# Recurrence of a hybrid encoder layer on one core: the two directions' 64x64 products placed in different quarters of the matmul array, alternating by units, and the outputs' first terms issued ahead of the state's update

## What is computed

```python
def rwkv7_step(S, inp):
    r, w, k, v, a, b = inp
    sa = jnp.einsum('dbhvk,dbhk->dbhv', S, a)
    S = S * w[..., None, :] + sa[..., None] * b[..., None, :] + v[..., :, None] * k[..., None, :]
    y = jnp.einsum('dbhvk,dbhk->dbhv', S, r)
    return S, y
...
    S0 = jnp.zeros((N_DIRS, B, H, N, N), jnp.float32)
    _, y = lax.scan(rwkv7_step, S0, xs)
    y = jnp.moveaxis(y, 0, 2)
    y = y[0] + jnp.flip(y[1], axis=1)
```

## Time and profile before

| | us |
|---|---|
| median of three runs | 3061.29 |
| lowest, highest | 3059.34, 3065.22 |
| profiled execution, first to last instruction (its span) | 3048.9 |

### The profile page before, as it was taken

The page is one execution under the profiler, slowest core; times in us unless marked ns, Lnnn a source line. Parts: engine busy times, 40 slices in busy tenths (PEclk is TensorE's granted clock), DMA queues, the critical chain, the costliest instruction groups (busy, mean ns, idle before and its releaser), DMA issues. The chain is left out here.

```text
span 3048.9 us, 62296 instructions
## 1 busy us (share of the span) xinstructions
PE 2789.9 (92%) x24610; PEld 2226.5 (73%) x24610; DVE 2058.0 (68%) x3096; ACT 1363.4 (45%) x2618; POOL 665.4 (22%) x843
## 2 busy tenths in 40 slices
PE   7889989998659999996999789999799999799999
PEld 4655578884459999994667678888588888588887
DVE  6867623235586666634446878888888888587786
ACT  4547711116635555543244434455444454344443
POOL 5447700000037787721232000000000000000000
PEclk9999999999869999998999899999899999899999
DMA  4432222324794444334654132222122221726401
GB/s 131 149 94 50 49 80 68 77 55 162 286 285 148 139 144 143 95 110 160 193 176 152 68 116 77 83 83 80 56 83 80 83 77 66 278 98 225 158 28 56
DMA packets 302490, 361.25 MB, mean 118 GB/s; under 512 B 119977, under 2 KB 202409, under 8 KB 302082
## 3 DMA queue, kind: packets, MB, share of 16 engines
q1 hardware_dynamic: 297314, 352.01, 35.6%
q10 hardware_dynamic: 4896, 5.38, 0.5%
HBM read 254.16 MB, written 103.14 MB: 117 GB/s over the span
## 5 line engine op out<-in xcount | busy, mean ns | idle before, releaser
L99 PE MATMUL up_p<-up_b_hi,up_a_hi 128*128 128x512 f32 x1232 | 490.3, 398 | 43.2 <-ACT inv L2295 23.3
L100 PE MATMUL up_p<-up_b_lo,up_a_hi 128*128 128x512 f32 x1232 | 490.1, 398 | 0.0
L101 PE MATMUL up_p<-up_b_hi,up_a_lo 128*128 128x512 f32 x1232 | 489.6, 397 | 0.0
L99 PEld LDWEIGHTS up_p<-up_b_hi,up_a_hi 128*128 128x128 f32 x1232 | 233.7, 190 | 103.7 <-ACT inv L2295 24.6
L100 PEld LDWEIGHTS up_p<-up_b_lo,up_a_hi 128*128 128x128 f32 x1232 | 233.6, 190 | 56.0
L101 PEld LDWEIGHTS up_p<-up_b_hi,up_a_lo 128*128 128x128 f32 x1232 | 233.5, 189 | 55.4
L2738 ACT CAST down_a_hi<-down_a 128x512 fp32r<-128x512 f32 x154 | 96.0, 623 | 259.5 <-PE down_p_x L101 143.4
L2250 ACT CAST up_a_hi<-up_a_sum 128x512 fp32r<-128x512 f32 x132 | 81.4, 617 | 224.3 <-DVE up_a_sum L2409 147.3
L2753 DVE TENSOR_TENSOR down_a_lo<-down_a,down_a_hi 128x512 fp32r<-128x512 f32 x154 | 106.3, 690 | 97.5 <-ACT down_a_hi L2738 97.5
L2320 ACT ACTIVATE up_con<-up_raw,vecs_sb 128x1023 f32<-128x1023 f32 (+1 forms) x88 | 109.7, 1246 | 127.4 <-DVE up_raw L2479 83.9
L2485 DVE SCALAR_TENSOR_TENSOR up_con<-up_raw,vecs_sb,up_con 128x1023 f32<-128x1023 f32 (+1 forms) x88 | 113.1, 1285 | 65.9 <-ACT up_con L2320 65.9
(11 more groups left out here) (298 smaller groups left out, 7356.9 us busy)
## 6 DMA issues: line engine op xcount, KB each, us to landing
up_a_raw<-in_w_up SPq DMA_DIRECT2D x172, 256.0 KB, 2.7
rec_inp<-gate_chunks SPq DMA_DIRECT2D x64, 512.0 KB, 3.7
down_a<-in_w_down SPq DMA_DIRECT2D x88, 256.0 KB, 8.7
down_b<-act_out SPq DMA_DIRECT2D x88, 256.0 KB, 9.0
first_w<-in_w_attn SPq DMA_DIRECT2D x24, 512.0 KB, 3.5
rkv_chunks<-rwkv_project_mix SPq DMA_DIRECT2D x12, 1024.0 KB, 6.5
gate_chunks<-gates_out SPq DMA_DIRECT2D x3, 4096.0 KB, 12.2
act_out<-up_con SPq DMA_DIRECT2D x22, 512.5 KB, 2.6
```

The costliest lines, as they stand in the source:

```text
L99: pe.matmul(out, w_hi, x_hi, start=start, stop=False, skip_group_check=True)
L100: pe.matmul(out, w_hi, x_lo, start=False, stop=False, skip_group_check=True)
L101: return pe.matmul(out, w_lo, x_hi, start=False, stop=stop, skip_group_check=True)
```

## The change

In PE's part of the recurrence `pair` gets an argument `across`, which exchanges the output's halves: partitions 0 to 63 in go to 64 to 127 out and the other way round, that is, to the two quarters off the diagonal. `x_part`, `u_part` and `gram` become `x_parts`, `u_parts` and `grams`: in each, direction 0 lies on the diagonal and direction 1 off it, and the directions alternate unit by unit. All waits of both directions stand ahead of the first matmul. `y_part` is cut in two: `y_given` (the terms from the values and from H) ahead of `h_part`, and `y_solved` (the term from u) behind it; here direction 0 lies off the diagonal and direction 1 on it. `tok_b_part` and `tok_part` become `tok_parts`, called with 0 ahead of `cross` and with 1 behind it: each call turns b of one direction (diagonal) and k of the other (off it), alternating. The semaphore `tok` is now `tok_k`, and `tok_copy` on ACT waits for both `tok_b` and `tok_k`. Since direction 0's outputs now come out with their halves exchanged, the mix loads them in two DMAs of 64 partitions in place of one of 128, and `sums` waits for three DMAs in place of two. The number and the shapes of the matmuls are the same, and the orders on ACT, DVE and POOL are as before.

```diff
-                def pair(to, lhs, rhs, start=True, stop=True):
-                    for rows in HALVES:
-                        mm = pe.matmul(to[rows], lhs[rows], rhs[rows], start=start, stop=stop)
+                def pair(to, lhs, rhs, start=True, stop=True, across=0):
+                    for h, rows in enumerate(HALVES):
+                        mm = pe.matmul(to[HALVES[h ^ across]], lhs[rows], rhs[rows], start=start, stop=stop,
+                                       skip_group_check=True)
                     return mm
...
-                def x_part(c, d):
...
+                def x_parts(c):
+                    for d in DIRS:
+                        done(pe, "ak_masked", d, c + 1)
+                        done(pe, parity("v", c), d, 48 * (c // 2 + 1))
+                        done(pe, "h_added", d, c)
+                        done(pe, "h_decayed", d, c)
                     for u in range(RU):
                         if c > 0:
-                            pair(to[:, u], ar[d][:, c % RING, u, 0:L], H[d][:, c % 2, u], True, False)
-                        mm = pair(to[:, u], akrk[d][:, c % 2, u, 0:L], vtok[d][:, c % 2, u], c == 0, True)
-                    mm.then_inc(S["x"][d], 1)
-                def u_part(c, d):
-                    done(pe, "merged", d, c + 1)
-                    done(pe, "x_copied", d, c + 1)
-                    each(bank[d][0][:, :, 0:L], Z[d], xs[d]).then_inc(S["u"][d], 1)
+                            for d in DIRS:
+                                pair(bank[d][0][:, u, 0:L], ar[d][:, c % RING, u, 0:L], H[d][:, c % 2, u], True,
+                                     False, across=d)
+                        for d in DIRS:
+                            mm = pair(bank[d][0][:, u, 0:L], akrk[d][:, c % 2, u, 0:L], vtok[d][:, c % 2, u],
+                                      c == 0, True, across=d)
+                            if u == RU - 1:
+                                mm.then_inc(S["x"][d], 1)
+                def u_parts(c):
+                    for d in DIRS:
+                        done(pe, "merged", d, c + 1)
+                        done(pe, "x_copied", d, c + 1)
+                    for u in range(RU):
+                        for d in DIRS:
+                            mm = pair(bank[d][0][:, u, 0:L], Z[d][:, u], xs[d][:, u], across=d)
+                            if u == RU - 1:
+                                mm.then_inc(S["u"][d], 1)
...
-                def y_part(c, d):
...
+                def y_given(c):
+                    for d in DIRS:
+                        done(pe, "merged", d, c + 1)
                     for u in range(RU):
-                        pair(to[:, u], vtok[d][:, c % 2, u], akrk[d][:, c % 2, u, L:], True, False)
+                        for d in DIRS:
+                            pair(bank[d][1][:, u, 0:L], vtok[d][:, c % 2, u], akrk[d][:, c % 2, u, L:], u == 0,
+                                 False, across=1 - d)
                         if c > 0:
-                            pair(to[:, u], H[d][:, c % 2, u], ar[d][:, c % RING, u, L:], False, False)
-                        for h, rows in enumerate(HALVES):
-                            mm = pe.matmul(to[rows, u], stacked[d][rows, c % 2, u, h], rb[d][rows, c % 2, u],
-                                           start=False, stop=True)
-                    mm.then_inc(S["y"][d], 1)
+                            for d in DIRS:
+                                pair(bank[d][1][:, u, 0:L], H[d][:, c % 2, u], ar[d][:, c % RING, u, L:], False,
+                                     False, across=1 - d)
+                def y_solved(c):
+                    for d in DIRS:
+                        done(pe, "rb_masked", d, c + 1)
+                        done(pe, "u_copied", d, c + 1)
+                    for u in range(RU):
+                        for d in DIRS:
+                            for h, rows in enumerate(HALVES):
+                                mm = pe.matmul(bank[d][1][HALVES[h ^ (1 - d)], u, 0:L],
+                                               stacked[d][rows, c % 2, u, h], rb[d][rows, c % 2, u],
+                                               start=False, stop=True, skip_group_check=True)
+                            if u == RU - 1:
+                                mm.then_inc(S["y"][d], 1)
...
-                def tok_b_part(c, d):
...
+                def tok_parts(c, b):
+                    k = 1 - b
+                    done(pe, "v_copied", b, NCH // 2)
+                    done(pe, "v_copied", k, NCH // 2)
+                    done(pe, "tok_copied", b, c)
+                    done(pe, "tok_copied", k, c)
+                    if b:
+                        done(pe, "tok_b", k, c + 1)
+                        done(pe, "tok_k", b, c + 1)
+                    to = [bank[d][3].rearrange("p u (j t) -> p u j t", j=2) for d in DIRS]
                     for u in range(RU):
                         for h, rows in enumerate(HALVES):
-                            mm = pe.matmul(to[rows, u, h], bt[d][rows, c % RING, u], ident[rows, rows], start=True,
-                                           stop=True)
-                    mm.then_inc(S["tok_b"][d], 1)
-                def tok_part(c, d):
...
+                            mm_b = pe.matmul(to[b][rows, u, h], bt[b][rows, c % RING, u], ident[rows, rows],
+                                             start=True, stop=True)
+                        if u == RU - 1:
+                            mm_b.then_inc(S["tok_b"][b], 1)
                         for h, rows in enumerate(HALVES):
-                            mm = pe.matmul(to[HALVES[1 - h], u, h], kt[d][rows, c % RING, u], ident[rows, rows],
-                                           start=True, stop=True)
-                    mm.then_inc(S["tok"][d], 1)
+                            mm_k = pe.matmul(to[k][HALVES[1 - h], u, h], kt[k][rows, c % RING, u], ident[rows, rows],
+                                             start=True, stop=True)
+                        if u == RU - 1:
+                            mm_k.then_inc(S["tok_k"][k], 1)
...
-                def gram(f, d):
...
+                def grams(f):
+                    for d in DIRS:
+                        done(pe, "ar", d, f + 1)
+                        done(pe, "b", d, f + 1)
+                        done(pe, "rb_masked", d, min(NCH, f - LAG + 2))
+                        done(pe, "g_copied", d, f)
+                    for u in range(RU):
+                        for d in DIRS:
+                            a, b = ar[d][:, f % RING, u, 0:L], bt[d][:, f % RING, u]
+                            lhs, rhs = (b, a) if d == 0 else (a, b)
+                            mm = pair(bank[d][2][:, u, 0:L], lhs, rhs, across=d)
+                            if u == RU - 1:
+                                mm.then_inc(S["gram"][d], 1)
...
                     now, ahead, front = live(c), live(c + 1), live(c + LAG)
-                    for go, stage, n in ((now, x_part, c), (ahead, ak_part, c + 1), (now, u_part, c),
-                                         (ahead, rb_part, c + 1), (now and c < NCH - 1, h_part, c),
-                                         (now, y_part, c), (ahead, tok_b_part, c + 1), (ahead, tok_part, c + 1),
-                                         (ahead, cross, c + 1), (front, gram, c + LAG),
-                                         (ahead, corner, c + 1)):
-                        if go:
-                            for d in DIRS:
-                                stage(n, d)
+                    if now:
+                        x_parts(c)
+                    if ahead:
+                        for d in DIRS:
+                            ak_part(c + 1, d)
+                    if now:
+                        u_parts(c)
+                    if ahead:
+                        for d in DIRS:
+                            rb_part(c + 1, d)
+                    if now:
+                        y_given(c)
+                    if now and c < NCH - 1:
+                        for d in DIRS:
+                            h_part(c, d)
+                    if now:
+                        y_solved(c)
+                    if ahead:
+                        tok_parts(c + 1, 0)
+                        for d in DIRS:
+                            cross(c + 1, d)
+                        tok_parts(c + 1, 1)
+                    if front:
+                        grams(c + LAG)
+                    if ahead:
+                        for d in DIRS:
+                            corner(c + 1, d)
...
                 def tok_copy(c, d):
-                    done(act, "tok", d, c + 1)
+                    done(act, "tok_b", d, c + 1)
+                    done(act, "tok_k", d, c + 1)
...
                     done(sp, "lo", n * KD)
-                    for d in range(2):
-                        sp.dma_start(flat(y[:, d]), K.y_dirs[d].rearrange("c p m -> p c m")[:, at]).then_inc(
+                    for h in range(2):
```

(6 more changed lines are left out.)

24 lines of the change are left out of this document (1 added, 23 removed).

## The result

The changed kernel takes 3105.57 us (median of four runs, 3105.32 to 3115.2), the kernel before 3062.35 us beside it: a ratio of 1.0142, interval 1.0128 to 1.0155. It is 43 us slower. The forecast was 20 us faster with a range up to 3078, so both the sign and the range were wrong. The profiled execution has a span of 3103.6 us at a mean granted clock of 0.936 (before: 3048.9 at 0.962). Most of the loss lies in the recurrence: 30 slots from the copy of the first outputs to that of the last but one took 449 us before and 485 after, 36 us more. One reading of the kernel before has to be set right: its span is 12.4 us under the median, and this was put down to what lies ahead of the first and behind the last instruction.

A forecast was written before the change was run, and what follows sets the result against it. The prediction took PE's own work to bound each recurrence slot. Gains of 16 us (24 slots) and 15 us (last slots), less 3 us of small parts and 8 us for the clock, gave 20 us faster, 3041, range 3016 to 3078.

The forecast's parts named there:

- Records at 16 ns: PE's alternating products in the recurrence: records over four quarters start every 16 ns in place of 29.
- part 1: The alternation's effect on PE's work: 288 records a slot at 13 ns less each, 3.8 us a slot.
- I leave the stalls as they are: PE's "issue" stalls in the recurrence, near 0.6 us a slot, were taken as unchanged.
- part 2: What is late next: slots laid out again through ACT and DVE, gaining 16 us in 24 slots, 15 in the last.
- An ordinary slot of 12.9: Recurrence slots other than fourth and last ones: 12.9 us each, against 14.2 before without the stall.
- cross_copy late: ACT's cross_copy before corner: PE, done with gram, waits 1.6 us for it in each ordinary slot.
- ak_mask late by 0.9: DVE's ak_mask, behind merge and scaled, holds up rb: PE waits 0.9 us in an ordinary slot.
- Fourth slots' wait for spread over 2 us: In each fourth slot cross waits over 2 us for spread, which needs turn_back on DVE; the slot takes 16.7 us.
- The clock: PE's granted clock falls in two or three of eight fourth slots, at most three places from 930 to 1380: 8 us lost.
- y_given ahead of h costs nothing: Moving y_given before h on PE is free, since the state is needed only at the next x, 5 us later.
- Last slots of 11.3: Last slots, without scaled, growth or gram: 11.3 us each against 13.4, 15 us gained over seven.
- the array or its issue doesn't feed four quarters for long: Rival, chance 0.12: PE's records start slower, at 29 ns 52 us slower (3113), at 25 ns 20 slower (3081, 0.06).

The follow-up runs named there:

- e1: Changed kernel with every product of x, u, y and gram back on the diagonal quarters, new order kept: 36 us slower than the kernel before (3099).
- e14: Changed kernel with both halves of the b and k products ahead of cross again, still alternating: 22 us faster than the changed kernel (3082).
- e13: Changed kernel with unread 256-column products in PE's two waits, array work in few instructions: 2 us less than the changed kernel, within its uncertainty.
- e15: Changed kernel with both b and k halves ahead of cross and without PE's implied waits: 26 us below e14, as fast as the kernel before.
- e10: Changed kernel without PE's waits that another wait already implies, 688 instructions less: 19 us faster than the changed kernel.
- e18: e14 with one product of y (H by ar, 64 instructions a slot) left out, so its outputs lack a part: 21 us less than e14.
- e11: Kernel before with only x, u and gram alternating in four quarters, and without PE's implied waits: 0.9953 of the kernel before, the study's fastest.

## Why the prediction was wrong

- **Records at 16 ns** (part 1): right, 16 ns in y_solved above, and x of both directions took 1.1 us.
- **"I leave the stalls as they are"** (part 2, the fourth slots): the step that failed. The 0.6 us a slot were PE waiting for code, and they depend on how fast the code is used up. They grew from 19.7 to 54.8 us in 450, or by 1.3 us for each of 30 slots: 39 of the 63 us between forecast and result, if each gap counts in full, which no run shows. That they grow with the array's speed is shown by e1 and the changed kernel: same order, gaps of 22.2 and 54.8 us. The prediction's own layouts of these two are 72 us apart (3113 at 29 ns, 3041 at 16 ns); measured, the fast one was 7 us slower. The burst in the earlier trace rows that I took as proof that the issue follows began at 929.45, and that is the first instruction of a block: it ran on code that had just arrived.
- **An ordinary slot of 12.9**: a second term that could not come true in 24 of 32 slots, since the loop through POOL takes 14.75 or more where the forecast's mean of four was 13.85. That alone is 0.9 x 24 = 22 us, all of the forecast gain. POOL's 77% in the earlier trace rows was read as slack, and its chain was not laid out; the work was in one piece of 50 us and the rest a chain.
- **cross_copy late**: right in kind, 1.2 us a slot against 1.6. That halving b and k around cross was a loss: right, 0.7 us a slot (e14) against the 0.8 by which the stretch was to grow. That the joint ends cost was right too: laid out at 29 ns, 52 us slower; e1 measured 36.
- **ak_mask late by 0.9**: wrong, 0.8 us in 22 slots; PE came later than laid out. **Fourth slots' wait for spread over 2 us**: 3.7 us in six waits, probably for the same reason.
- **The clock**: at most three drops forecast, 28 low stretches found between 930 and 1417, so the number was far off. Whether its price (8 us) was too low is not shown: e13 took away more than half of the low time for 2 us, but its fill has a cost of its own.
- **y_given ahead of h costs nothing**: not shown alone; with the joint ends the y part cost 14 us.
- **Last slots of 11.3**: the last four full ones took 13.5 to 16.4 (before 13.2 to 14.0), in e15 11.3 to 13.6.

The rival "the array or its issue doesn't feed four quarters for long" named the right place and 3113 us, at 0.06. That it is near the 3106 measured is in part luck: the array did feed four quarters at 16 ns, and what came to about 29 ns a pair at best was the arrival over eight blocks. The slot average of the changed kernel was higher, 4.6 us a block.

The parts by themselves: x, u and gram -4, y +14, both with b and k alternating +22, the b and k products halved around cross +43. The changed kernel also has 134 waits more that are instructions (1672 against 1538), an estimated 4 us at the 28 ns of e10. What stays open is how the 63 us divide among block gaps, the low clock (131 us low from 930 to 1380, 31 in e1, 10 before) and single waits; they trade against each other, and no run fixes one of them alone.

## What to carry to other kernels

Where small products follow each other on PE, count its instructions, and not the array's time alone: here blocks of 256 never started to arrive less than 3.29 us apart, and over eight blocks took 3.63 us or more each, 26 to 29 ns for a pair of load and product. Products packed into four quarters, at 16 ns, can't be kept up over several blocks, and each wait that stood as an instruction of its own cost 18 to 45 ns. Look also at what a new order costs without the packing: here 36 of the 43 us. When a profile says "issue" at places without a wait, number the instructions; gaps at equal distances are code that has not arrived. Of an engine at 77%, ask in how long a piece its work comes and what stands between two pieces, before taking the rest as slack.

## What the hardware showed beyond this

- 64 by 64 products in four quarters start every 15 to 17 ns, for 32 records (0.52 us) and for the 64 of x (1.1 us). Records can start ahead of earlier ones of the program: in the changed kernel two of x at 1086.61, the last two of corner at 1086.70.
- Two blocks of PE's code never started to arrive less than 3.29 us apart, in 20 kernels of different load.
- With 82 of 360 us at 1.2 GHz (e18) the slots were as long as with 17 us (e11), 15.0 us, where the loop through POOL set the pace.
- Changing between transposes and products on PE costs 0.18 and 0.25 us, each time.
